# The second token block in reversed order in a hybrid decoder block's mixer, and one stationary operand for both blocks at each recurrence level

## What is computed

```python
h    = rms_norm(x, ln_mix_w)
proj = h @ w_in                    # 2048 x 9216: u_pool | q | f | i | g | gate_a | gate_b
y_a  = multiscale_pool(u_pool, pool_mix_w, pool_scale) @ w_branch_a
y_b  = hgrn2(q, f, i, g, lb, hgrn_norm_w) @ w_branch_b       # 8 heads of 128
x    = x + (sigmoid(gate_a) * y_a + sigmoid(gate_b) * y_b) @ w_out
u    = causal_depthwise_conv(rms_norm(x, ln_ffn_w) @ w_up, conv_w, conv_b)
x    = x + (silu(u_gate) * u_val) @ w_down
x    = x + sigmoid(rms_norm(x, ln_ple_w) @ w_ple_gate) * (p @ w_ple)
return rms_norm(x, ln_final_w)

# hgrn2, per head, b = cumulative sum over time of log f, k = 1 - f:
# o[t] = sum over s <= t of  (q[t] * exp(b[t] - b[s])) . k[s]  *  v[s]
```

## Time and profile before

| | |
|---|---|
| time, median of 3 runs | 1458.8 us (1458.59 to 1458.89) |
| the profiled execution | 1459.32 us |
| its span | 1457.3 us |
| TensorE matmul busy | 1446.8 us, 99% of the span |
| VectorE, ScalarE, GpSimd busy | 908.4, 740.4, 144.3 us |
| granted TensorE clock | 0.999 |
| DMA | 273.97 MB, mean 188 GB/s |

### The profile page before, as it was taken

One profiled execution on the slowest core, in us unless ns is written; L12 is line 12 of the kernel. 1 busy time (PEld: TensorE's weight loads), 2 busy tenths in 40 slices (PEclk: granted clock), 3 DMA queues, 4 the chain that ended last, 5 costly groups with the idle time before them and its releaser, 6 DMA issues.

```text
span 1457.3 us, 19697 instructions
## 1 busy us (share of the span) xinstructions
PE 1446.8 (99%) x7268; PEld 1231.3 (84%) x7268; DVE 908.4 (62%) x1032; ACT 740.4 (51%) x886; POOL 144.3 (10%) x72
## 2 busy tenths in 40 slices
PE   9999999999999999999999999999999999999997
PEld 7888888888888888888888888888888888888886
DVE  7577676545454555566777777777777555454655
ACT  7545645444444444555555555555555444343544
POOL 0053053000000000001101111011011000000000
PEclk9999999999999999999999999999999999999999
DMA  8765555556666655566566565665665665555653
GB/s 313 246 184 147 167 150 159 145 173 188 191 190 197 188 192 184 181 183 190 177 200 188 179 201 180 193 190 181 192 192 182 204 201 190 185 190 190 219 198 120
DMA packets 190873, 273.97 MB, mean 188 GB/s; under 512 B 11616, under 2 KB 103136, under 8 KB 190688
## 3 DMA queue, kind: packets, MB, share of 16 engines
q1 hardware_dynamic: 190528, 273.08, 59.6%
q10 hardware_dynamic: 288, 0.11, 0.0%
HBM read 271.04 MB, written 2.10 MB: 187 GB/s over the span
## 4 chain that ended last, share of the span: by engine, by line
PE 98%; issue 0%; DMA 0%; DVE 0%; ACT 0%; SPq 0%; ACTq 0%; POOLq 0%; POOL 0%; DVEq 0%
PE main L552 20%; PE main L554 20%; PE main L553 20%; PE aux L608 11%; PE main L608 11%; PE aux L617 6%; PE main L617 6%; PE aux L682 2%; PE aux L648 1%; PE aux L716 0%; DMA raw<-in_w_in 0%; PE aux L665 0%; PE aux L706 0%; PE aux L696 0%; PE aux L695 0%
## 5 line engine op out<-in xcount | busy, mean ns | idle before, releaser
L1111 DVE TENSOR_TENSOR w_lo<-raw,w_hi 128x1024 fp32r<-128x1024 f32 (+1 forms) x500 | 623.2, 1255 | 490.1 <-ACT w_hi L859 488.9
L859 ACT ACTIVATE w_hi<-raw 128x1024 fp32r<-128x1024 f32 (+1 forms) x500 | 525.0, 1053 | 595.4 <-PE main L554 409.5
L552 PE MATMUL main<-w_hi,xT 128*128 128x512 f32 x702 | 276.8, 394 | 0.7 <-DVE xT L1138 0.7
L554 PE MATMUL main<-w_hi,xT 128*128 128x512 f32 x702 | 273.4, 389 | 0.0
L553 PE MATMUL main<-w_lo,xT 128*128 128x512 f32 x702 | 273.3, 389 | 0.0
L608 PE MATMUL aux<-xT,w_hi 128*128 128x512 f32 x704 | 169.8, 391 | 0.0
L608 PE MATMUL main<-xT,w_hi 128*128 128x512 f32 x672 | 163.0, 391 | 0.0
L552 PEld LDWEIGHTS main<-w_hi,xT 128*128 128x128 f32 x702 | 131.9, 188 | 27.8 <-DVE xT L1138 1.1
L554 PEld LDWEIGHTS main<-w_hi,xT 128*128 128x128 f32 x702 | 131.7, 188 | 27.7
L553 PEld LDWEIGHTS main<-w_lo,xT 128*128 128x128 f32 x702 | 131.9, 188 | 26.2
L608 PEld LDWEIGHTS aux<-xT,w_hi 128*128 128x128 f32 x704 | 129.3, 188 | 25.3 <-issue 0.3
(11 more groups left out here) (187 smaller groups left out, 1370.1 us busy)
## 6 DMA issues: line engine op xcount, KB each, us to landing
raw<-in_w_up SPq DMA_DIRECT2D x336, 256.0 KB
raw<-in_w_in SPq DMA_DIRECT2D x136, 512.0 KB
raw<-in_w_down SPq DMA_DIRECT2D x84, 512.0 KB
raw<-in_w_out SPq DMA_DIRECT2D x32, 512.0 KB
raw<-in_w_ple_gate SPq DMA_DIRECT2D x32, 512.0 KB
raw<-in_w_branch_a SPq DMA_DIRECT2D x16, 512.0 KB
raw<-in_w_branch_b SPq DMA_DIRECT2D x16, 512.0 KB
raw<-in_w_in SPq DMA_DIRECT2D x16, 256.0 KB, 5.6
```

What stands on the lines that cost most here:

```text
L552: pe.matmul(acc, th, wh, start=first, stop=False)
L554: return pe.matmul(acc, tl, wh, start=False, stop=end)
L859: ac.activation(w_hi[:, u % RING, :, 0:w], raw[:, u % RING, :, 0:w], ACT.Copy).then_inc(hi_full, 1)
L1111: dve.tensor_tensor(w_lo[:, u % RING, :, 0:w], raw[:, u % RING, :, 0:w], w_hi[:, u % RING, :, 0:w].bitcast(F32), ALU.subtract).then_inc(lo ...
```

## The change

Tokens 128 to 255 are stored in reversed order from `x_t` on until `mT`, whose transposes turn them back (`in_time`). In a reversed block the later half of a stretch lies left. So at a level the keys of block 0 fill the left halves of a 128-column tile and those of block 1 the right halves of the same tile; `dec` becomes 4 heads by 128 key columns and 4 heads by 128 query columns. Per head one matmul with 128 moving columns takes the place of two with 64. It also computes pairs of one block with the other, which no pick reads.

```diff
 score_level (TensorE)
-                    for t in range(TB if l < 8 else 1):
-                        a = h * SEQ + t * P
-                        if l < 8:
-                            o, n = (2 * h + t) * (P // 2), P // 2
-                            right = halves(e[:, a:a + P], HALVES[l - 1])[:, :, 1, :]
...
+                    o = h * P
+                    if l < 8:
+                        left, right = e[:, o:o + P], e[:, 4 * P + o:4 * P + o + P]
+                    else:
+                        left, right = e[:, h * SEQ:h * SEQ + P], e[:, h * SEQ + P:(h + 1) * SEQ]
+                    mm = pe.matmul(flat[:, o:o + P], left, right, start=True, stop=True)
 exponents (VectorE)
-                    dve.tensor_tensor(ev[:, :, 0, :], ref, bv[:, :, 0, :], ALU.subtract)
-                    dve.tensor_tensor(ev[:, :, 1, :], bv[:, :, 1, :], ref, ALU.subtract).then_inc(arg_ready, 1)
+                    dve.tensor_tensor(keys[:, :, :, 0, :], ref0, b0[:, :, :, 0, :], ALU.subtract)
+                    last_op = dve.tensor_tensor(keys[:, :, :, 1, :], ref1, b1[:, :, :, 1, :], ALU.subtract)
+                    if l > 1:
+                        dve.tensor_tensor(queries[:, :, :, 1, :], b0[:, :, :, 1, :], ref0, ALU.subtract)
+                        last_op = dve.tensor_tensor(queries[:, :, :, 0, :], b1[:, :, :, 0, :], ref1, ALU.subtract)
 the scan (VectorE)
-                    dve.tensor_tensor_scan(bT_flat, scan_keep[:], bT_flat, 0.0, ALU.mult, ALU.add).then_inc(b_ready, 1)
+                    for h in range(4):
+                        for tb in range(TB):
+                            b = bT[:, h, in_time(tb)]
+                            last_op = dve.tensor_tensor_scan(b, scan_keep[:], b, 0.0, ALU.mult, ALU.add)
 decay, level 1 (ScalarE)
-                    ac.activation(halves(e, CHUNK)[:, :, 0, :], halves(e, CHUNK)[:, :, 0, :], ACT.Exp)
-                    ac.activation(halves(e, CHUNK)[:, :, 1, :], halves(bT_flat, CHUNK)[:, :, 1, :],
-                                  ACT.Exp).then_inc(dec_ready, 1)
+                    ac.activation(e[:, 0:4 * P], e[:, 0:4 * P], ACT.Exp)
+                    ac.activation(queries[:, :, :, 1, :], b0[:, :, :, 1, :], ACT.Exp)
+                    ac.activation(queries[:, :, :, 0, :], b1[:, :, :, 0, :], ACT.Exp).then_inc(dec_ready, 1)
 the products (GpSimd), levels 1 to 7
-                    pool.tensor_tensor(e[:, :, 0, :], e[:, :, 0, :], halves(kT_flat, m)[:, :, 0, :], ALU.mult)
-                    pool.tensor_tensor(e[:, :, 1, :], e[:, :, 1, :], halves(qT_flat, m)[:, :, 1, :], ALU.mult).then_inc(qk_ready, 1)
+                        for tb in range(TB):
+                            to = keys[:, :, :, tb, :]
+                            pool.tensor_tensor(to, to, k[tb][:, :, :, tb, :], ALU.mult)
+                            to = queries[:, :, :, 1 - tb, :]
+                            last_op = pool.tensor_tensor(to, to, q[tb][:, :, :, 1 - tb, :], ALU.mult)
 pick (VectorE), levels 1 to 7
-                dve.copy_predicated(right, mask, data).then_inc(sc_ready, 1)
+                for tb in range(TB):
...
+                    last_op = dve.copy_predicated(to, mask, data[:, :, :, 1 - tb, :])
 transposes (TensorE)
+                        at = in_time(tb) if name[:2] == "mT" else slice(tb * P, (tb + 1) * P)
+                        mm = pe.transpose(dst[:, b, at], src(b, tb), ident[:])
```

More of the change, by code:

```diff
@@ L247, in build @@
         g_tok = sb("g_tok", [P, TB, NCOL], F32, hg)
[L248 to L249 removed]
+        scan_keep = sb("scan_keep", [P, P], F32, hg)
+        levels = sb("levels", [P, len(HALVES), 2, P // 2], F32, hg)
         band = sb("band", [P, 4, 3 * P], F32, hg)
@@ L365, in cols, with in_time, groups, keys_and_queries @@
             return slice(n * NCOL, (n + 1) * NCOL)
+        def in_time(tb):
+            return slice(2 * P - 1, P - 1, -1) if tb else slice(0, P)
+        def groups(ap, m):
+            return ap.rearrange("p h (n a m) -> p h n a m", a=2, m=m)
+        def keys_and_queries(l):
+            e = dec[:, l % 2, :].rearrange("p (k h t) -> p k h t", k=2, h=4)
+            return [groups(e[:, k], HALVES[l - 1]) for k in range(2)]
+        def first_and_second(t, l):
+            return [groups(t[:, :, tb * P:(tb + 1) * P], HALVES[l - 1]) for tb in range(TB)]
         def halves(ap, m):
@@ L1485, in _ @@
                     pool.wait_ge(dec_ready, 8 * g + l)
[L1486 to L1489 removed]
+                    if l < 8:
+                        (keys, queries), k, q = keys_and_queries(l), first_and_second(kT, l), first_and_second(qT, l)
+                        for tb in range(TB):
[3 more added lines that the diff above has]
+                            last_op = pool.tensor_tensor(to, to, q[tb][:, :, :, 1 - tb, :], ALU.mult)
+                        last_op.then_inc(qk_ready, 1)
+                    else:
+                        e = halves(dec[:, l % 2, :], P)
+                        pool.tensor_tensor(e[:, :, 0, :], e[:, :, 0, :], halves(kT_flat, P)[:, :, 0, :], ALU.mult)
+                        pool.tensor_tensor(e[:, :, 1, :], e[:, :, 1, :], halves(qT_flat, P)[:, :, 1, :], ALU.mult).then_inc(qk_ready, 1)
                 pool.wait_ge(o_ms, g + 1)
@@ L1520, in laid_out @@
     conv = np.concatenate([v["conv_w"][0], v["conv_b"]], 0).reshape(4, 2 * KF, P)
-    return {"x": v["x"], "x_t": v["x"][0].T.reshape(KD, P, SEQ).transpose(1, 0, 2),
+    turned = np.concatenate([v["x"][0, 0:P], v["x"][0, :P - 1:-1]], 0)
+    return {"x": v["x"], "x_t": turned.T.reshape(KD, P, SEQ).transpose(1, 0, 2),
             "p_t": v["p"][0, 0].T.reshape(2, P, SEQ).transpose(1, 0, 2),
@@ L1530, in shape_constants @@
     s, t = np.arange(P)[:, None], np.arange(P)[None, :]
-    masks = [((s // (2 * m) == t // (2 * m)) & (s % (2 * m) < m))[:, np.arange(P) % (2 * m) >= m] for m in HALVES]
+    masks = []
+    for m in HALVES:
+        same, left = s // (2 * m) == t // (2 * m), s % (2 * m) < m
+        masks.append(np.stack([(same & left)[:, np.arange(P) % (2 * m) >= m], (same & ~left)[:, np.arange(P) % (2 * m) < m]], 1))
     S, T = np.arange(SEQ)[:, None], np.arange(SEQ)[None, :]
```

44 lines of the change are left out of this document (17 added, 27 removed).

## The result

| | before | after |
|---|---|---|
| median | 1458.89 us, 11 executions (1458.59 to 1459.50) | **1462.52 us**, 11 executions (1459.80 to 1463.52) |
| ratio after to before | | **1.0021, 95% interval 1.0013 to 1.0029** |
| the profiled execution | 1459.32 us | 1459.80 us |
| its span | 1457.3 us | 1457.7 us |
| granted TensorE clock in it | 0.999 | 0.998 |

The changed kernel is slower by 3.6 us, 0.25%. The profiled execution is its fastest one, only 0.5 us above that of before. So there are two things to explain: why the 11 us taken off TensorE are not seen, and what the other executions have that the profiled one has not.

A forecast was written before the change was run, and what follows sets the result against it. TensorE was taken to bound 98% of the span, its saving capped by a closed loop of the other engines. 2 x 2.1 of delay - 3.5 + 0.3 gave +1.0 us; forecast 1459.8 us, range 1453 to 1467.

The forecast's parts named there:

- dearer products: Rival: GpSimd product pieces cost more than 0.72 us; slower from 0.76 on, 1466.6 us at 0.85; chance 0.38.
- Matmuls, 1.70 to 0.80: TensorE at levels 2 to 7: 8 records replace 16, saving 0.90 us each; with level 1, 5.7 us a group.
- The cap of 3.5 us: Level 8's products have 2.5 and 1.0 us of slack in the two groups, so the gain is at most 3.5 us.
- The rival by which all of it shows: Rival: TensorE's whole 11.4 us saving shows in the time, 1447.4 us; chance 0.04.
- the one by which the matmuls get no cheaper: Rival: levels stay at 1.70 us on TensorE and the loop still moves, 1459.9 us; chance 0.03.
- X: Delay of GpSimd's products from split scan, exponents, exp and products: 2.1 us a group, paid in both groups.
- GpSimd pieces of 0.72: Products k and q at a level: four operations of 256 elements replace two of 512, each 0.72 us when unblocked.
- The exponents queue behind q1: VectorE's next exponents wait for GpSimd's last product piece, part of +0.1 us a period; rival without queueing 1453.1, chance 0.09.
- Waits of TensorE: TensorE waits for the q product from level 5 or 6 (group 0), 4 or 5 (group 1): 12 us in sum.
- the loop of 7.1 to 7.3: VectorE, ScalarE and GpSimd cycle from one level's exponents to the next: 7.1 to 7.3 us in place of 6.97.
- has room: The period with the g_tok stores was taken to absorb the dearer pieces at levels 6 and 7 (1.52 at 107.49).
- The second way to level 8: Level 7's last product ends 1.2 us later, then TensorE needs 6.37; with TensorE's restarts put at 0.15 us a group.

The follow-up runs named there:

- the kernel with the filled wait: Changed kernel with ten unused f32 identity matmuls before TensorE's wait for level 7's products, both groups: 1459.70 us, ratio 1.0005 to the kernel before.
- TensorE's part alone: Kernel before with four matmuls of 128 moving columns per group at every level, all that feeds them unchanged: 1455.12 us, ratio 0.9974.
- the merged version: Changed kernel with qT, kT, bT stored block by block, so exponents, products and scan are two operations each: 1456.17 us, ratio 0.9981 to the kernel before.

## Why the prediction was right, and where it was not

The time, 1462.5, lies 2.7 above the forecast of 1459.8, inside the range, and the ratio puts it on the border of what the text called no change, on the slower side. The mechanism of the forecast held and one cost was missing. At full clock the sum was good: 0.9 us slower (the kernel with the filled wait, and the one fast execution, against the medians of before) where it said 1.0. That the range also holds the median is in part luck: it reached up to 1467 for dearer products, not for the clock.

- **Matmuls, 1.70 to 0.80.** Right, and level 1 too: its matmuls now start 0.81 us ahead of the next unit (79.09 to 79.90), and the 0.3 assumed for it fits the 1.07 us of before (79.52 to 80.59).
- **The cap of 3.5 us.** Right, and the main point. TensorE's part alone gave 3.8, out of 11. The rival by which all of it shows is refuted by the same run, as is the one by which the matmuls get no cheaper.
- **X, 2.1 us a group.** Right: 2.17 and 2.07. From the start of the scan to the end of level 8's last product it takes 61.82 us in group 0, before 59.65, and 61.80 against 59.73 in group 1:

```profile
66.92 2.63 DVE L1259 TENSOR_TENSOR_SCAN bT<-scan_keep,bT 128x128 f32<-128x128 f32 x8
...
126.46 2.28 POOL L1515 TENSOR_TENSOR dec<-dec,qT 128x512 f32<-128x512 f32 x1
```

  The terms are less even than assumed. Scan +0.35 (2.63, before 2.28), assumed 0.5; its two-operation form in the merged version takes 2.33, so walking backwards costs nothing that shows. Exp at level 1 +0.1: the next split starts 1.15 us after the first exp (71.50 to 72.65), as assumed. Loop, assumed +0.24 a period: +0.26 to +0.31 in the four from level 2 to 6, +0.67 in the one with `g_tok`, but 0.25 and 0.38 less in the first and the last. Level 8's exponents, put at nothing, take 0.64 more for their first two operations (1.39, before 0.75), which queue behind q1 of level 7. That the sum fits so well is in part luck.
- **GpSimd pieces of 0.72.** 0.73, and 1.7 beside a split. The rival of dearer products needed 0.76 or more; only the pieces of levels 6 and 7 are (0.86), and the forecast had named these.
- **The exponents queue behind q1.** Right: 0.96 for the first operation, 0.41 when q1 is left out.
- **Waits of TensorE, "under 1 us each and 12 us in sum".** The sum, 9.4, is inside the 8 to 16 given. They begin at level 3 in group 0 and level 2 in group 1, where the text had 5 or 6 and 4 or 5. The played-through period had the reason: q1 ends 4.93 us behind ScalarE's split in place of 3.69 (measured 4.96, 87.19 to 92.15). The text counted that for level 7 only, but it makes the product of every level up to 7 late. "Under 1 us each" failed: level 7 waits 2.50 in both groups. The step at fault is the loop of 7.1 to 7.3 taken for all levels. The text had let the period of `g_tok` go as one that "has room". It has 8.70 us between exponents (8.03 before), against 6.37 of TensorE: room in VectorE's and GpSimd's queues, but the longest period of all on the chain. A stretch that has room for the added work is still the one where TensorE, made faster, waits longest.
- **The second way to level 8**, from level 7 through TensorE: put at 0.15 a group, "about equal". It was the one that decided, but by little, since level 8 starts without a wait, 6.45 us after level 7, and its own last product had ended 0.3 us before it (128.74 against 129.03). Counted from the diagonal matmuls, level 8 of group 0 came 0.37 us earlier than before (57.18 us behind them against 57.55; at 129.03 and 129.74, the 129.52 of the earlier trace rows being the weight load ahead of it), where 0.25 was forecast from 2.5 - 2.1 - 0.15; group 1 then lost 1.04 against it, where 1.1 plus 0.15 was forecast. That makes +0.7 against +1.0 predicted; the span shows +0.4, since the execution of before had started 0.34 late.
- **The clock.** Missing altogether. A half-speed stretch behind a 2.5 us wait costs 1.6 us, and by its time and clock the median execution on the first chip had two. That, not X, is nearly all that lies between +0.9 us (the fastest execution against the median of before) and +3.6 us (the median). The forecast priced a wait as its length. The "slower" side got its 0.38 for dearer products; the slowdown came by another way.

Open: why the half-speed stretch comes after some waits of 2.5 us and not after others of the same length, and why most executions had one of them on one chip and most two on the other. In the profile of the merged version the waits of 1.96 and 1.99 us had none behind them; its other clocks suggest that some of its executions had one, and no trace of these was taken. Open too is why some profiles reach the diagonal matmuls of group 0 up to 1.3 us later than others (71.51 to 72.77).

## What to carry over

When a saving on the bounding engine ends in waits, look at the schedule before giving it up: here 3.8 of 11 us came with the matmuls alone, and 9.8 once the producers' loop had been given more units and its operations put together again. Before splitting an operation of a producer into one per block, see whether another storage order makes it one access: that was worth 5.2 us here. Find the longest period of the producers' loop, not the usual one, since there TensorE will wait longest, and price a wait of some microseconds with what its clock loses behind it. Before two traces are subtracted, align them at the last point ahead of the change: here X reads as 1.8 us without that and 2.1 with it, the loss as 0.4 and 0.7.

## What the hardware showed unexpectedly

- A TensorE wait of 2.52 us was followed by 3.4 us at a granted clock of 0.50, in the middle of a kernel that is otherwise at 1.00; it cost 1.6 us. A second wait of 2.52 us in the same execution, and two of 2.50 us in another of the same kernel, were followed by none. With 20 records of ident matmuls in the wait, eleven executions of eleven lay within 0.72 us at a mean clock of 0.998 to 0.999. With waits of 1.4 us at most, eight of eight lay within 0.3 us at the same clock.
- A GpSimd multiplication of 256 elements takes 0.73 us, and 0.86 where the runs are of one or two elements (levels 6 and 7); two of them cost 1.46 where one of 512 costs 1.28 to 1.30, crossing access or not.
- A scan cut in eight pieces of 128 takes 2.63 us, in two of 512 (one backwards) 2.33, in one of 1024 2.28: 0.05 us for each cut, less than the 0.07 of a plain subtraction.
